# Two latent chunks and the spatial weights turned by DVE, a whole first chunk of x, and two changed orders

## What is computed

```python
# first block
h = rms_norm(x, g_pre)
q_lat, kv_lat, k_rope, gate_mla, fq, fk, fv, f_logit, gate_fox = split(h @ w_in)  # q_lat 768 wide, kv_lat 512
q  = rms_norm(q_lat, g_q) @ w_uq       # up-projections of the latents
kv = rms_norm(kv_lat, g_kv) @ w_ukv
o_mla = causal_attention(q, kv, k_rope) * silu(gate_mla)      # 8 heads
o_fox = forgetting_attention(fq, fk, fv, f_logit) * silu(gate_fox)   # 8 heads
x = x + rms_norm(concat(o_mla, o_fox) @ w_out, g_post)
# second block
x = x + 0.5 * swiglu(rmsnorm(x), ffn1)
h = rmsnorm(x); q, k, v, u, vs, g_att, g_sg = split(h @ w_in_2)
vs = layernorm(gelu(vs))
w_sp = sg_w * causal                   # sg_w: 12 groups of 128 x 128 spatial weights
spatial = einsum('gts,bcsgd->bctgd', w_sp, vs) + sg_b
y_sg = (gelu(u) * spatial) @ w_sg_out
x = x + (sigmoid(g_att) * y_att + sigmoid(g_sg) * y_sg) @ w_out_2
x = x + 0.5 * swiglu(rmsnorm(x), ffn2)
```

## Time and profile before

| | |
|---|---|
| runs | 2627.14, 2628.66, 2628.70 us, median 2628.66 |
| profiled execution | 2629.09 us, of which the span of the core's work is 2627.3 us |
| busy in the span | PE 99%, PE weight loads 82%, DVE 57%, ACT 45%, POOL 7% |
| DMA | mean 210 GB/s |

### The profile page before, as it was taken

One profiled execution on the slowest core, in us unless ns is written; L12 is line 12 of the kernel. 1 busy time (PEld: TensorE's weight loads), 2 busy tenths in 40 slices (PEclk: granted clock), 3 DMA queues, 4 the chain that ended last, 5 costly groups with the idle time before them and its releaser, 6 DMA issues.

```text
span 2627.3 us, 32024 instructions
## 1 busy us (share of the span) xinstructions
PE 2610.1 (99%) x11781; PEld 2167.2 (82%) x11781; DVE 1493.0 (57%) x1700; ACT 1186.7 (45%) x1349; POOL 174.8 (7%) x292
## 2 busy tenths in 40 slices
PE   9999999999999999999999999999999999999998
PEld 8888888788888888888888888888888888888886
DVE  6755665755555555556555665555655555555554
ACT  5544554444444444444444554444454444444333
POOL 0110000000000000001100310000100000000000
PEclk9999999999999999999999999999999999999999
DMA  7876666577777776667876477665777777777664
GB/s 215 251 236 194 209 208 192 158 219 215 219 216 218 217 217 210 209 210 255 241 220 187 148 217 217 208 208 192 232 216 215 219 216 220 217 216 226 195 188 152
DMA packets 277138, 552.87 MB, mean 210 GB/s; under 512 B 21978, under 2 KB 24888, under 8 KB 276792
## 3 DMA queue, kind: packets, MB, share of 16 engines
q1 hardware_dynamic: 257520, 489.88, 61.3%
q0 software_dynamic: 19024, 61.54, 7.8%
q10 hardware_dynamic: 504, 0.26, 0.0%
HBM read 521.70 MB, written 29.89 MB: 210 GB/s over the span
## 4 chain that ended last, share of the span: by engine, by line
PE 97%; DVE 1%; ACT 1%; DMA 0%; issue 0%; SPq 0%; DVEq 0%; ACTq 0%
PE acc L548 95%; PE s_ps L680 1%; PE tr L592 1%; PE o_ps L703 1%; DVE wlo L1360 0%; DMA raw<-in_w_in 0%; PE tr L915 0%; DVE act_lo L1392 0%; ACT whi L974 0%; DVE stats L1452 0%; ACT kv L1200 0%; DVE o_sb L1783 0%; ACT L1200 0%; ACT o_hi L1031 0%; DVE xres L1864 0%
## 5 line engine op out<-in xcount | busy, mean ns | idle before, releaser
L1360 DVE TENSOR_TENSOR wlo<-raw,whi 128x1024 fp32r<-128x1024 f32 x929 | 1129.9, 1223 | 992.5 <-ACT whi L974 988.2
L974 ACT ACTIVATE whi<-raw 128x1024 fp32r<-128x1024 f32 x929 | 978.5, 1057 | 1162.9 <-PE acc L548 1137.3
L548 PE MATMUL acc<-whi,act_hi 128*128 128x512 f32 (+1 forms) x2560 | 692.6, 392 | 4.1 <-DVEq L1400 2.6
L548 PE MATMUL acc<-wlo,act_hi 128*128 128x512 f32 (+1 forms) x2560 | 683.3, 389 | 0.0
L548 PE MATMUL acc<-whi,act_lo 128*128 128x512 f32 (+1 forms) x2560 | 683.2, 389 | 0.0
L548 PEld LDWEIGHTS acc<-wlo,act_hi 128*128 128x128 f32 x2560 | 480.1, 188 | 100.0
L548 PEld LDWEIGHTS acc<-whi,act_lo 128*128 128x128 f32 x2560 | 479.7, 188 | 100.4
L548 PEld LDWEIGHTS acc<-whi,act_hi 128*128 128x128 f32 x2560 | 473.1, 188 | 97.6 <-DVEq L1400 3.4
L548 PE MATMUL acc<-whi,h_lo 128*128 128x512 f32 x704 | 188.3, 389 | 0.0
L548 PE MATMUL acc<-wlo,h_hi 128*128 128x512 f32 x704 | 188.3, 389 | 0.0
L548 PE MATMUL acc<-whi,h_hi 128*128 128x512 f32 x704 | 188.3, 389 | 0.0
(11 more groups left out here) (257 smaller groups left out, 1372.4 us busy)
## 6 DMA issues: line engine op xcount, KB each, us to landing
raw<-in_w_in SPq DMA_DIRECT2D x280, 512.0 KB, 4.4
raw<-in_ffn_w_gate SPq DMA_DIRECT2D x176, 512.0 KB, 4.4
raw<-in_ffn_w_up SPq DMA_DIRECT2D x176, 512.0 KB, 4.2
raw<-in_ffn_w_down SPq DMA_DIRECT2D x176, 512.0 KB, 4.6
raw<-in_w_out SPq DMA_DIRECT2D x64, 512.0 KB, 4.6
turn_dram<-h_turned POOLq DMA_DIRECT2D x25, 512.0 KB, 3.2
h_back<-turn_dram POOLq DMA_DIRECT2D x100, 128.0 KB, 5.5
raw<-in_w_sg_out SPq DMA_DIRECT2D x24, 512.0 KB, 4.4
```

The source lines that it names most:

```text
L548: return nc.tensor.matmul(pair[:, half, 0:width], left[:, k, half * P:(half + 1) * P], right[:, slot, t, 0:width], start=start, stop=stop, ...
L974: nc.scalar.activation(whi[:, slot, :, 0:width], raw[:, slot, :, 0:width], ACT.Copy).then_inc(hi_ready, 1)
L1360: nc.vector.tensor_tensor(wlo[:, slot, :, 0:width], raw[:, slot, :, 0:width], whi[:, slot, :, 0:width].bitcast(F32), ALU.subtract).then_in ...
```

## The change

Five edits. (1) `ident` is read from ACT's queue ahead of `gain_rows`, no longer from SP's, and the first chunk of x comes in one DMA instead of two. (2) Latent chunks 0 and 1 are turned by DVE and exchanged; ACT and DVE split what comes back at group 7 of the second and third unit, ahead of the copy-out there. The last two tiles are still turned by PE. (3) `FOX_STEPS`: even heads have probs after group +4 and values after +5, together with the next head's scores; odd heads stay as they were. (4) In the first FFN's opening DVE's `post_chunk(3)` moves from group 2 to group 3, behind the split of chunk 2, and `keep_warm(4)` is `keep_warm(3)`. (5) sg_w is read in four DMAs, in squares of 32, turned by one DVE instruction, and multiplied by the triangle in one.

```diff
-             for d, step in ((4, "values"), (1, "scores"), (3, "probs"))]
+             for d, step in ((1, "scores"), (4 - h % 2, "probs"), (5 - h % 2, "values"))]
+FOX_STEPS.sort(key=lambda s: (s[0], s[1] != "values"))
...
-            sp.dma_start(fix[:, 0:P], fixed[:, 0:P]).then_inc(ident_in, 16)
             for k in range(G_D):
-                if k == 0:
-                    for part, landed in enumerate((x_first, x_in[0])):
-                        cols = slice(part * (W // 2), (part + 1) * (W // 2))
-                        sp.dma_start(xres[:, :, cols], x[:, cols].rearrange("(h p) n -> p h n", p=P)).then_inc(landed, 16)
-                elif k < CHUNKS:
+                if k < CHUNKS:
...
+            for i in range(2):
+                exchange(EX_LAT + i, lat_turned, lat_back[i])
...
-            pool.dma_start(wsp_raw, sg_w_2.rearrange("g t s -> t g s")).then_inc(wsp_in, 16)
+            squares = sg_w_2.rearrange("g (a i) (b j) -> b i (g a) j", i=QUAD, j=QUAD)
+            for b in range(QUADS):
+                pool.dma_start(wsp_raw[b * QUAD:(b + 1) * QUAD, :].rearrange("p (m j) -> p m j", j=QUAD),
+                               squares[b]).then_inc(wsp_in, 16)
...
             for j in groups(G_D, act_hi, act_lo):
-                if j == 3:
-                    transpose_chunk(lat, 0)
+                pass
             for j in groups(G_D, act_hi, act_lo, LAT2):
-                if j == 3:
-                    transpose_chunk(lat, W)
+                if j == 7:
+                    exchanged()
...
                     if (c, j) == (0, 0):
+                        at.n["ready"] += 1
                         transpose_chunk(lat, 2 * W, 2)
+                    if (c, j) == (0, 1):
+                        pe.wait_ge(chunk_split, at.n["chunk"])
+                        at.n["chunk"] += 1
...
-                    keep_warm(4)
+                    keep_warm(3)
...
-                    if c == 0 and j in (1, 3, 5):
-
-                        g = 4 * (j // 2)
-                        pe.wait_ge(wsp_in, 16)
-                        job([(P, slice(i * P, (i + 1) * P), wsp_raw[:, g + i, :]) for i in range(4)])
...
+            act.dma_start(fix[:, 0:P], fixed[:, 0:P]).then_inc(ident_in, 16)
             act.dma_start(gain_rows[:], gains_by_row).then_inc(rows_in, 16)
...
                 if j == 7:
+                    at.n["turn"] = EX_LAT
+                    turned_hi(lat_hi, 0, lat_back[0], GAINS["lat"])
+                    at.n["ready"] += 1
                     copy_out(lat, slice(W, 2 * W), "pre")
...
-                if j == 3:
-                    chunk_lo(lat_hi, lat_lo, 4, GAINS["lat"] + 4)
                 if j == 7:
+                    turned_lo(lat_hi, lat_lo, 4, lat_back[1], GAINS["lat"] + 4)
+                    at.n["ready"] += 1
                     copy_out(lat, slice(2 * W, LAT), "pre", LAT2)
...
-                    if first_one and j == 2:
+                    if first_one and j == 3:
                         post_chunk(3)
...
+                    if (c, j) == (0, 1):
+
+                        dve.wait_ge(wsp_in, 16 * QUADS)
+                        settled(nc.vector.transpose(wsp_turned.rearrange("p (m i) -> p m i", i=QUAD),
+                                                    wsp_raw.rearrange("p (m j) -> p m j", j=QUAD)))
+                    if (c, j) == (0, 3):
+                        nc.vector.tensor_tensor(wspT[:], wsp_turned.rearrange("p (g t) -> p g t", g=SG_GROUPS),
+                                                tri.unsqueeze(1).to_broadcast([P, SG_GROUPS, P]),
+                                                ALU.mult).then_inc(wsp_ready, 1)
```

More of the change, by code:

```diff
@@ L92 @@
               + 15 * G_D + CHUNKS * (2 * G_D + 2 + 6) + CHUNKS * G_D)
-EX_MLA, EX_FOX, EX_O = 0, 5, 9
+EX_LAT, EX_MLA, EX_FOX, EX_O = 0, 2, 7, 11
 EX_FFN1 = EX_O + CHUNKS - 1
@@ L234, in build @@
         late = [place_at(f"late{i}", [P, CHUNK], F32, q_at + (12 + 4 * i) * 1024)[0] for i in range(5)]
+        lat_turned, lat_back = fox[:, 1, 2 * FOX:2 * FOX + CHUNK], [kv[:, 0, i * CHUNK:(i + 1) * CHUNK] for i in range(2)]
         mla_turned = [fox[:, 0, 0:CHUNK], fox[:, 1, 0:CHUNK], fox[:, 0, FOX:FOX + CHUNK],
@@ L264, in build @@
         vs2, top = place_at("vs2", [P, HALVES, SG_W], F32, top)
-        wsp_raw = u2[:, :, :].rearrange("p h n -> p (h n)")[:, 0:SG_W].rearrange("p (g s) -> p g s", g=SG_GROUPS)
+        flat_u = u2[:, :, :].rearrange("p h n -> p (h n)")
+        wsp_raw, wsp_turned = flat_u[:, 0:SG_W], flat_u[:, SG_W:2 * SG_W]
         top_of_att = top
@@ L324, in build @@
         tr_free = [sem(f"tr_free{i}") for i in range(2)]
-        x_first = sem("x_first")
         x_in = [sem(f"x_in{c}") for c in range(CHUNKS)]
@@ L602, in transpose_chunk @@
                     if from_input is not None:
-                        pe.wait_ge(x_first if (from_input, b) == (0, 0) else x_in[from_input], 16)
+                        pe.wait_ge(x_in[from_input], 16)
                     elif by_part:
@@ L910, in spatial @@
                 if b == 0:
-                    pe.wait_ge(wsp_ready, 3)
+                    pe.wait_ge(wsp_ready, 1)
                     pe.wait_ge(ln_done, HALVES * SG_W // W)
@@ L1118, in _ @@
             for j in groups(G_D):
-                if j == 3:
-                    chunk_hi(lat_hi, 0, GAINS["lat"])
                 if j == 4:
@@ L1129, in _ @@
                     take_root("q")
-                if j == 3:
-                    chunk_hi(lat_hi, 4, GAINS["lat"] + 4)
                 if j == 7:
+                    turned_hi(lat_hi, 4, lat_back[1], GAINS["lat"] + 4)
+                    at.n["ready"] += 1
                     copy_out(lat, slice(2 * W, LAT), "pre", LAT2)
@@ L1274, in _ @@
                 for j in groups(G_D):
-                    if c == 0 and j in (1, 3, 5):
-                        at.n["job"] += 1
                     for where, step, h, g in MIX_STEPS:
@@ L1288, in _ @@
                         if c == 3:
-                            act.wait_ge(wsp_ready, 3)
+                            act.wait_ge(wsp_ready, 1)
                         activate((vs2 if c < 3 else u2)[:, :, c % 3 * W:(c % 3 + 1) * W], ACT.Gelu, "mix")
@@ L1605, in _ @@
                     for c in (2 * j - 8, 2 * j - 7):
-                        if c == 0:
-                            dve.wait_ge(x_first, 16)
                         dve.wait_ge(x_in[c], 16)
@@ L1617, in _ @@
                     dve.sem_inc(chunk_ready, 1)
+                    turn_chunk(lat_turned, lat[:, :, 0:W])
             sin, cos = angle[:, 2], angle[:, 3]
@@ L1642, in _ @@
                                             ALU.min, ALU.max).then_inc(angle_ready, 1)
-                if j == 3:
-                    chunk_lo(lat_hi, lat_lo, 0, GAINS["lat"])
                 if j == 7:
+                    at.n["turn"] = EX_LAT
+                    turned_lo(lat_hi, lat_lo, 0, lat_back[0], GAINS["lat"])
+                    at.n["ready"] += 1
                     copy_out(lat, slice(W, 2 * W), "pre")
@@ L1648, in _ @@
                     dve.sem_inc(chunk_ready, 1)
+                    turn_chunk(lat_turned, lat[:, :, W:2 * W])
             for j in groups(G_D):
@@ L1993, in _ @@
                 for j in groups(G_D):
-                    if c == 0 and j in (1, 3, 5):
-                        bank = at.n["job"] % 2
-                        g = 4 * (j // 2)
-                        dve.wait_ge(tr_done, at.n["job"] + 1)
-                        last = nc.vector.tensor_tensor(wspT[:, g:g + 4, :], tr[bank][:].rearrange("p (g t) -> p g t", g=4),
-                                                       tri.unsqueeze(1).to_broadcast([P, 4, P]), ALU.mult)
-                        last.then_inc(tr_free[bank], 1)
-                        dve.wait_ge(tr_free[bank], at.n["job"] // 2 + 1)
-                        dve.sem_inc(wsp_ready, 1)
-                        at.n["job"] += 1
+                    if (c, j) == (0, 1):
[6 more added lines that the diff above has]
+                                                ALU.mult).then_inc(wsp_ready, 1)
                     for where, step, h, g in MIX_STEPS:
```

## The result

The changed kernel took **2632.39 us** in the median of 20 runs (2631.05 to 2633.51), the kernel before 2628.39 in 20 runs beside it (2627.11 to 2629.53): a ratio of 1.0016, 95% interval 1.0009 to 1.0022. It is slower by 4.0 us, less than the 0.2% set as bound, so "within 0.2%" in the prediction's terms, but the forecast was 1.5 us faster. The profiled execution took 2632.07 us with a span of 2630.3, 3.0 above the span before.

The account below looks back on a forecast made before the run. The prediction took PE, busy for 99% of the span, as the bound. Its terms, -1.8 + 3.5 + 1.6 - 1.9 - 1.2 - 1.4 - 0.3 = -1.5, took 2628.66 to 2627.2 us, range 2622.5 to 2632.5.

Parts of the forecast that it names:

- The start: Kernel start: fewer SP issues win at most 0.6 us, gain_rows may be late; -0.3 us, bounds -0.6 and +0.4.
- The latent wait: Before the last two latent tiles: PE waits for the copy-out behind chunk 1's low parts on DVE; +3.5 us.
- The clock behind it: After PE's wait at the latents: granted clock of 0.50 for some 3.3 us, costing half of it; +1.6 us.
- Rival (a): Last latent tiles: exchange and loads are quick, PE waits 0.9 us, the clock holds; 2623.0 us, chance 0.15.
- Rival (b): Latents: the exchange comes late, near its long end, 6 us more wait; 2633 us, chance 0.10.
- Transposes: Latent chunks 0 and 1: PE no longer turns them, 0.9 us per eight transposes; -1.8 us.
- first FFN: First FFN's opening: moving post_chunk(3) starts group 4 earlier, PE's waits become 1.0 and 1.5 us; -1.9 us.
- forgetting heads: Forgetting heads: two waits of 0.40 us and one of two interruptions go; -1.2 us, bounds -0.8 and -1.3.
- spatial weights: Spatial weights: PE is spared four transposes, 0.46 us, in each of three jobs; -1.4 us.
- rival (c): First FFN's opening: the clock falls after all, 1.6 us more; 2628.8 us, chance 0.13.
- Rival (d): Spatial weights: their read in 128-byte pieces holds up the loads, PE waits 7 us; 2635.8 us, chance 0.12.

Follow-up runs that it names:

- E1: The changed kernel with gain_rows issued first and ident second on ACT's queue; 2632.03 us.
- E2: The changed kernel with ident read first on SP's queue again, gain_rows alone on ACT's, first chunk of x still whole; 2630.55 us.
- E11: The kernel before with the start edit alone: ident on ACT's queue ahead of gain_rows, first chunk of x whole; 2631.16 us.
- E7: The changed kernel with latent chunks turned by PE again and ident first on SP's queue; 2624.23 us.
- E8: The kernel of E7 with only latent chunk 0 exchanged, PE asking for its parts at the third unit's start; 2626.00 us.
- E10: The kernel of E8 with PE asking for chunk 0's parts after group 3 of the third unit; 2623.65 us.
- E12: The kernel of E10 with the start of the kernel before: first chunk of x in halves, ident first on SP's queue; 2623.24 us.
- E5: The changed kernel with the exchange of latent chunk 1 moving a few rows, not its megabyte, the rest a constant; 2629.25 us.
- E6: The changed kernel with keep_warm(40) ahead of PE's wait for the last latent unit; 2633.92 us.
- E9: The changed kernel with keep_warm(20) ahead of PE's wait for the last latent unit; 2630.26 us.
- E3: The changed kernel with the two latent chunks turned by PE again, both exchanges out; 2626.81 us.
- E4: The changed kernel with PE's turning of the last two latent tiles moved behind the fourth group of w_uq; 2627.34 us.

## Why the prediction was wrong

**The start (-0.3 forecast, +2.8 in the profile).** This is the step that gave the wrong sign. I had written that `gain_rows` "may be up to a microsecond late" and bounded the edit by +0.4. PE went on with it 2.0 us late. Its issue was only 0.5 us later, but a half megabyte of x was then issued ahead of it (0.76) and one of weights right behind it (1.25); the trace of before showed `gain_rows` only in the first place of its queue, and I took that landing for its own. The pace of PE had no term in this part of the sum at all: PE was still waiting when, in the kernel before, it reached full pace, and it ran at half pace up to 13. E1, E2 and E11 show the late read, the spacing of PE's starts the pace. Nor did the sum have a term for the whole first chunk of x, which it took for a gain: once the small reads were in time PE waited for it, 0.66 us in E2 and 1.65 to 1.89 in E7, E8 and E10, and without that wait E12 begins its second set of w_in 1.3 us sooner than E10.

**The latent wait (+3.5 forecast, 5.05).** The mechanism and its order held: DVE late by chunk 0's subtractions and the turning, the third load of w_uq freed late, the low parts ahead of the copy-out. The working gave 77.8 less 73.9, 3.9 us, of which 3.5 was taken; that is 0.4 of the 1.55 missing. That load was to be freed at 67.3 on the time scale of before; the changed kernel runs 1.9 behind it at this place, so 69.2, and it was issued at 68.86. The mis-sized term is the landing, 4.3 us with 0.8 added for the exchange; it took 7.1. E5 shows that 1.6 to 1.7 of it are the exchange's bytes.

**The clock behind it (+1.6 forecast, 1.9).** Right in kind and nearly in size for this execution; E6 and E9 show it apart from the wait. It is no fixed price: behind the waits of E2 and E5 it was 2.6. Rival (a), a wait of 0.9, did not come. Rival (b) put the lateness into the exchange; ACT used what the exchange brought at 76.98, behind the split of the third load, and the exchange was not the last to come.

**Transposes (-1.8 forecast, -1.77), first FFN (-1.9, -1.91), forgetting heads (-1.2, -1.48), spatial weights (-1.4, -1.41).** All held. In the first FFN the two waits are 0.98 and 1.29 us, where 1.0 and 1.5 were written down, at full clock: rival (c) falls.

**Rival (d), 128-byte pieces.** The four reads of 192 KB were issued from 1197.68 to 1202.58 and landed 4.9 to 6.3 us after their issue, 5.2 in the median; the one read of 768 KB before had taken 6.5. The last was issued at about 1201.7, so the whole took, by an estimate from these numbers, 9 to 10 us: 2.4 to 3.8 more, where the rival needed over 6. ACT waited 1.66 and 1.85 us for two loads, and PE for none. The Trainium skill ("DMA: Bandwidth & Descriptors", Specifications) asks for 512 bytes or more for line rate. This trace does not show that the shorter runs cost PE anything; what they cost the read itself it does not separate from POOL's issues, which take 0.9 us each. Two readings in the rival's working were off as well: 15 us of missing loads less 7 of lead are 8, not 7, and the high part at 1206.31 was late mainly because ACT split a chunk of the left operand from 1204.35 on. It waited for its data for 0.39 us.

In sum: +3.1 from the start and +1.9 from the latents, less 0.5 that the rest gained more, are the 4.5 between the forecast of -1.5 and the +3.0 of the profiled execution. The median lies a further microsecond up; what differs from run to run is not settled for the changed kernel, but the profiled executions differ in the start, by the wait for `gain_rows` (1.6 to 3.3 us) and by when PE comes to full pace. The median, 2632.39, is still inside the range of 2622.5 to 2632.5. That is luck: the range was made wide for the rivals, none of which came, and the start was not among them.

## What to carry to other kernels

At a kernel's start a small read that the first instruction needs is worth a place ahead of every large one; issued half a microsecond later it let PE go on two later, and the half pace behind PE's wait cost 0.7 more. When work moves from PE to an exchange through DMA, price the loads beside it anew: the bytes of the exchange lengthen the loads that the next stage waits for. Where a chunk has slack (chunk 0, E10) the exchange gained nearly what it saved, 0.8 of 0.9 us. With the second chunk as well, whose parts stand ahead of a copy-out that PE needs at once, the two cost 7.0 us and saved 1.8. Chunk 1 alone was not tried, so how much of the 7.0 needs both is open.

## What the runs showed that I had not expected

The same start gave other waits and another pace. Three cases can be told apart by the starts of PE's matmuls on ones, 0.21 or 0.11 us apart, and by the granted clock.

| case | kernel: idle time of PE before it turns the gains or x, in us | full pace first reached | behind the wait |
|---|---|---|---|
| full pace came and stayed | E9: 1.61; E11: 1.65; E7: 1.65 | 5.0; 5.4; 4.0 | full pace, the 14 matmuls take 1.73 us |
| full pace came, then fell | E8: 1.85; E10: 1.89; E3: 2.36; E4: 3.26 | 4.9; 4.1; 4.1; 4.7 | clock 0.50 from 8.3 to 11.7; 7.5 to 10.9; 7.5 to 10.9; 8.1 to 11.6; the 14 matmuls take 2.87; 3.20; 2.81; 2.39 |
| the wait came before full pace | E5: 1.70; changed kernel: 1.83; E1: 2.00; E6: 2.65 | 13.0; 13.1; 12.9; 10.6 | half pace up to then, the 14 matmuls take 3.20 us, in E6 2.14 |

A longer wait did not cost more in step: PE's second set of w_in started at 13.41 in the changed kernel, 13.44 in E1 and 13.35 in E4, after waits of 1.8, 2.0 and 3.3 us. And the length of the wait alone does not tell what follows: behind 1.65 us PE ran at full pace in E11, and behind 1.70 at half pace in E5. In E11 the rise is recorded at 5.35, when PE had already stood idle since 5.22; what decides whether it comes is open. A granted clock that reads 1.00 ahead of its first record says nothing, as in the changed kernel, E1 and E5 up to 13 us; the spacing and length of like instructions are the surer sign.
